# Nine operations stand elsewhere in their engines' sequences, in the recurrence rounds of a fused pool and RWKV block

## What is computed

```python
def rwkv7_branch(ps, mu, ...):
    xs = ps + (token_shift(ps) - ps) * mu
    r, k, v, xw, xa, xg = jnp.split(xs, SHIFT_SPLITS, axis=-1)
    w = -jax.nn.softplus(-(w0 + jnp.tanh(xw) @ w_decay_up)) - 0.5
    decay = jnp.exp(-jnp.exp(w.astype(jnp.float32)))
    a = jax.nn.sigmoid(a0 + xa @ w_aaa_up)
    kk = heads(k * k_k);  kk = kk / jnp.maximum(norm(kk), 1e-12)
    k = k * (1 + (a - 1) * k_a)
    o = wkv7_scan(rh, heads(decay), kh, vh, kk, heads(a))
    ...

def step(state, inp):                      # wkv7_scan, one token
    r_t, w_t, k_t, v_t, a_t, b_t = inp     # a_t = -kk, b_t = kk * a
    sa = jnp.einsum('bhvk,bhk->bhv', state, a_t)
    state = (state * w_t[:, :, None, :] + sa[..., None] * b_t[:, :, None, :]
             + v_t[..., None] * k_t[:, :, None, :])
    return state, jnp.einsum('bhvk,bhk->bhv', state, r_t)
```

## Time and profile before

| what | value |
|---|---|
| time, median of 3 runs | 1096.57 us (1090.94 to 1103.49) |
| the profiled execution's own time | 1097.87 us |
| its span, first to last instruction | 1096.1 us |
| PE busy | 995.9 us (91%) |
| VectorE busy | 520.8 us (48%) |
| ScalarE busy | 413.7 us (38%) |
| GpSimd busy | 402.4 us (37%) |
| mean granted TensorE clock | 0.963 of full |

### The profile page before, as it was taken

One profiled execution on the slowest core, in us unless ns is written; L12 is line 12 of the kernel. 1 busy time (PEld: TensorE's weight loads), 2 busy tenths in 40 slices (PEclk: granted clock), 3 DMA queues, 4 the chain that ended last, 5 costly groups with the idle time before them and its releaser, 6 DMA issues.

```text
span 1096.1 us, 25425 instructions
## 1 busy us (share of the span) xinstructions
PE 995.9 (91%) x10997; PEld 798.7 (73%) x10997; DVE 520.8 (48%) x620; ACT 413.7 (38%) x500; POOL 402.4 (37%) x236
## 2 busy tenths in 40 slices
PE   1798999798989899899899999899999999999992
PEld 1676777685768578766688888678888888888881
DVE  5735688466837867853431246745112112112217
ACT  0336355345435623335432224384124224214311
POOL 6332512310231131125454444355444444443422
PEclk9698999998999999999999999889999999999996
DMA  9332333233222423422443543304333333333201
GB/s 363 103 90 62 97 102 100 61 83 119 86 79 80 119 65 99 116 86 59 135 115 87 165 123 96 96 5 130 97 96 97 96 96 96 96 96 96 77 1 77
DMA packets 153641, 108.08 MB, mean 99 GB/s; under 512 B 5395, under 2 KB 145601, under 8 KB 153537
## 3 DMA queue, kind: packets, MB, share of 16 engines
q1 hardware_dynamic: 143729, 83.46, 26.0%
q10 hardware_dynamic: 9808, 23.08, 6.9%
HBM read 100.23 MB, written 2.10 MB: 93 GB/s over the span
## 4 chain that ended last, share of the span: by engine, by line
PE 75%; DVE 14%; ACT 3%; DMA 2%; issue 2%; POOL 1%; ACTq 1%; SPq 1%; DVEq 0%; POOLq 0%
PE set L1773 23%; PE bank L1773 20%; PE bank L1476 12%; PE set L1518 3%; PE set L1530 2%; PE set L1542 2%; PE bank L1457 2%; PE set L1554 1%; PE bank L1875 1%; DMA ptab<-in_mu_shift_dram 1%; DVE y L1280 1%; DVE Q L1038 1%; PE set L1565 1%; DVE Q L1057 1%; PE set L1875 1%
## 5 line engine op out<-in xcount | busy, mean ns | idle before, releaser
L560 POOL TENSOR_TENSOR w_lo<-w_raw,w_hi 128x1024 fp32r<-128x1024 f32 (+2 forms) x87 | 201.7, 2318 | 441.2 <-ACT w_hi L641 401.1
L616 POOL TENSOR_TENSOR w_lo<-w_raw,w_hi 128x1024 fp32r<-128x1024 f32 x48 | 115.8, 2412 | 145.6 <-ACT w_hi L942 145.4
L1476 PE MATMUL bank<-h_hi,w_hi 128*128 128x512 f32 x256 | 109.3, 427 | 2.2 <-POOL w_lo L560 2.0
L669 ACT ACTIVATE Q<-set 128x1024 f32<-128x1024 f32 x56 | 57.4, 1025 | 135.1 <-PE set L1530 75.6
L641 ACT ACTIVATE w_hi<-w_raw 128x1024 fp32r<-128x1024 f32 (+2 forms) x75 | 75.5, 1006 | 83.0 <-PE set L1773 43.5
L942 ACT ACTIVATE w_hi<-w_raw 128x1024 fp32r<-128x1024 f32 x60 | 63.7, 1061 | 110.7 <-PE bank L1773 53.9
L1476 PE MATMUL bank<-h_lo,w_hi 128*128 128x512 f32 x256 | 104.1, 407 | 0.0
L1476 PE MATMUL bank<-h_hi,w_lo 128*128 128x512 f32 x256 | 103.5, 404 | 0.6 <-issue 0.6
L1371 DVE TENSOR_TENSOR f<-t 128x512 f32<-128x512 f32 x32 | 26.3, 823 | 125.6 <-ACT t L951 125.2
L1773 PE MATMUL set<-y_hi,w_hi 128*128 128x512 f32 x192 | 76.2, 397 | 0.0
L1773 PE MATMUL bank<-h_hi,w_hi 128*128 128x512 f32 x192 | 75.9, 395 | 0.0
(11 more groups left out here) (338 smaller groups left out, 2028.7 us busy)
## 6 DMA issues: line engine op xcount, KB each, us to landing
w_raw<-in_w_ff_dram SPq DMA_DIRECT2D x64, 512.0 KB, 3.9
w_raw<-in_w_in_dram SPq DMA_DIRECT2D x46, 512.0 KB, 3.8
y<-in_w_ada_dram ACTq DMA_DIRECT2D x20, 512.0 KB, 4.2
ada<-in_w_ada_dram SPq DMA_DIRECT2D x16, 512.0 KB, 10.0
Q<-in_w_ada_dram ACTq DMA_DIRECT2D x12, 512.0 KB, 4.3
w_raw<-in_w_rwkv_up_dram SPq DMA_DIRECT2D x8, 512.0 KB, 4.1
w_raw<-in_w_out_dram SPq DMA_DIRECT2D x8, 512.0 KB, 4.0
xtok<-in_x_dram SPq DMA_DIRECT2D x4, 512.0 KB, 10.0
```

What stands on the lines that cost most here:

```text
L560: link(pool.tensor_tensor(part_of(k, w_lo), part_of(k, w_raw), part_of(k, w_hi).bitcast(F32), ALU.subtract), "lo_ready")
L616: again(pool.tensor_tensor(part_of(k, w_lo), part_of(k, w_raw), part_of(k, w_hi).bitcast(F32), ALU.subtract), "lo_ready")
L669: link(act.activation(by_half(tile), psum_flat(set_of(name)), ACT.Copy), "act_kept")
L1476: mm = pe.matmul(o, w, hx, start=(m == 0), stop=(m == 3 * KT - 1))
```

## The change

Nothing is computed otherwise; nine operations move.

- ScalarE: the copy of D goes from slot 10 to slot 9, ahead of the square root L808 and of the fourth load. The issue of the fifth load of w_ada (block 4) goes from the end of slot 11 into slot 12, behind `lora_tanh` and ahead of the copy of K.
- VectorE: A8T plus one goes from slot 8 to slot 7, ahead of the shift and a small copy. `scaled_writes(n, 1)` goes from slot 18 to slot 19, behind the two MR sums. The shift of slot 22 goes to slot 24, behind the fourth state step's add. The use of the last block of w_ada goes from slot 18 to slot 26, behind the last state step's add. One pooling step of round 3 (group 1, last step) goes from slot 6 to slot 7.

```diff
-        ADA_LOADED = (1, 5, 7, 9, 11, 12, 14, 15)
-        ADA_USED = (4, 8, 10, 11, 13, 14, 16, 18)
+        ADA_LOADED = (1, 5, 7, 9, 12, 12, 14, 15)
+        ADA_MIDDLE = 4
+        ADA_USED = (4, 8, 10, 11, 13, 14, 16, 26)
...
-        for g, at in enumerate(((2, 3), (4, 5, 6), (8, 9, 10, 11), (12, 13, 14, 15, 16))):
+        for g, at in enumerate(((2, 3), (4, 5, 7), (8, 9, 10, 11), (12, 13, 14, 15, 16))):
...
+            def load_ada(it, kt):
+                tile = KT * it + kt
+                if it or ada_before(kt):
+                    act.wait_ge(sem("ada2_used"), KT * it + ada_before(kt))
+                if kt == 2:
+                    wait_made(act, "D1", it)
+                act.dma_start(ada_tile(kt), w_ada[0, (tile % KT) * P:(tile % KT + 1) * P, (2 + it) * D:(3 + it) * D]).then_inc(sem(f"ada2_in{int(kt in (2, 4, 6))}"), 16)
...
+                if s == 9 and work:
+                    keep(b6, "D", it)
                 if s == 9 and tail and it < QUADS:
                     act.wait_ge(sem("o_var"), it)
                     link(act.activation(gn[:, 2, :], gn[:, 1, :], ACT.Sqrt), "o_std")
...
-                if s == 10:
-                    if work:
-                        keep(b6, "D", it)
-                    if prep:
-                        squares(it, 1)
+                if s == 10 and prep:
+                    squares(it, 1)
                 if s == 12:
                     if prep:
                         lora_tanh(it, 1)
                     if work:
+                        load_ada(it, ADA_MIDDLE)
                         keep(b1, "K", it)
...
-                if work and s in ADA_LOADED:
-                    kt = ADA_LOADED.index(s)
...
+                if work and s in ADA_LOADED and s != 12:
+                    load_ada(it, ADA_LOADED.index(s))
+                if work and s == 12:
+                    load_ada(it, ADA_MIDDLE + 1)
...
-                at = {1: -1, 7: 0, 10: 1, 16: 2, 18: 3, 22: 4}
+                at = {1: -1, 7: 0, 10: 1, 16: 2, 18: 3, 24: 4}
...
-                if s in (0, 1, 10, 18, 22):
+                if s in (0, 1, 10, 18):
                     if s == 18 and work:
                         keep_pair(b1, b2, "AP1", it)
                     project(it, s)
-                    if s == 18 and prep:
-                        scaled_writes(n, 1)
...
                     if work:
                         keep_masked(c6, c8, mKR, "KR0", it)
                         keep_masked(c6, c8, mKR, "KR1", it)
+                        keep_plus_one(b5, "A8T", "A8T", it)
                     project(it, s)
                     if prep:
                         chunk_decay(n, 0)
-                if s == 8:
-                    if work:
-                        keep_plus_one(b5, "A8T", "A8T", it)
...
                     keep_sums(b4, b6, b4, Rt, "MR0", it)
                     keep_sums(b4, b6, b4, Rt, "MR1", it)
+                if s == 19 and prep:
+                    scaled_writes(n, 1)
...
                     keep(dve.tensor_tensor(state, ps, state, ALU.add), f"S{at}", it)
+                if s == 24:
+                    project(it, s)
```

## The result

The changed kernel takes 1089.73 us (median of 20 runs, 1083.93 to 1097.95); the kernel before took 1097.68 beside it. The ratio is 0.9934, interval 0.9913 to 0.9954: 7 us faster, not 22. One of the 20 executions of the kernel before took 1707.8 us; why is not known, and the ratio is of the others. The profiled execution took 1089.25 us with a span of 1087.5, so 8.6 are to be explained between it and the one shown of before.

A forecast was written before the change was run, and what follows sets the result against it. PE's list was taken to bound rounds 0 to 3, with only its idle time and low-clock stretches to win; 5.7, 8.0, 5.5 and 3.1 us by round make 22.3, so 1097.9 becomes 1076, range 1067 to 1088.

The forecast's parts named there:

- D's copy and the load: ScalarE, rounds 0 to 2: yT 5.4 us earlier in round 1 (3.0 if the clock drops), 3.55 in round 2.
- A8T ahead of the shift: VectorE, rounds 0 to 2: A8T comes 0.95 us earlier for PE's inv0; gain 0.9, 0.5 and 1.0 us.
- MR sums: VectorE, rounds 0 to 2: sums taken once MR0 is made, OI follows N unwaited; 6.6 us in three rounds.
- `rt_made` held by GpSimd: Ahead of S1's add: GpSimd's product holds the pair once a round, 3.00 us instead of 1.4.
- The shift: State steps S1 to S6, rounds 0 and 1: gain 3.2 and 3.7 us, less 0.9 if low clock comes.
- Round 2: Whole round: 3.55 us, then 5.95 at S1's add, less 0.4, so 5.5 us faster.
- Round 3: Pooling step behind A8T (W0 2.2 us earlier), no 1.86 before K, but yT waits for KI: 3.1 us faster.
- (b): Rival: half given back, `rt_made` held by both products (6.0 us), state steps at low clock (4.5); 1086, chance 0.15.
- (c): Rival: waits hide another bound, such as VectorE's list in slots 14 to 20; 1089, chance 0.07.

The follow-up runs named there:

- the second execution: The changed kernel, unaltered, measured and profiled once more: 1090.15 us, ratio 0.9927 to the kernel before; its profiled time was 1080.71 us.

## Why the prediction was wrong

**The step that failed** is in its first paragraph: "only two things can be won there, PE's idle time [...] and stretches at the low clock", with each wait then booked as won in full, as in "OI follows N with no wait: 1.84 us in this round, 6.6 in three". There was a third term, PE's supply of instructions: 12.5 us over the four rounds in the profiled execution, 8.2 in the second. It stood in the rows of before at 7.6 us, as idle for issue in the midst of products, and I read it as part of the idle time and not as a limit that sits behind the data waits. Taking the waits away brought it up.

- **D's copy and the load.** Right: HD1's wait is 1.27 (predicted 1.1), twice, and KI's new wait before yT 0.87 (predicted 0.8). 2.4 us a round each. The run with this part alone is as fast as the whole change, though only 2.4 us of it show as less idle time.
- **A8T ahead of the shift.** inv0 no longer waits for it; round 0 has 0.54 and round 2 0.85 for issue close by, round 1 nothing.
- **MR sums.** The wait went; the gain didn't come. In round 2, 2.47 for the sums became 2.45 for issue. The run with this part alone, 0.9998, shows that this term of 6.6 us was worth 2.7 us at the very most (0.9975).
- **`rt_made` held by GpSimd.** Wrong, and in my favour: 3.0 us a pair was expected, and it took 1.4 in all three rounds. GpSimd's products wait for OI, OI ended later than in my timetable because of its stalls (without the 0.38 and 1.36 of round 1 the product would have started at 285.9, inside `rt_made`), and VectorE was through. Timelines of VectorE and GpSimd of after, round 1 and round 0:

```profile
285.56 1.42 DVE L1266 TENSOR_TENSOR Q<-G 128x512 f32<-128x512 f32 x2
```

```profile
192.20 2.31 POOL L594 TENSOR_TENSOR Q<-Q,DC 128x1024 f32<-128x1024 f32 x1 [5.14 <-PE set L1535]
```

  In round 0 `rt_made` starts at 191.33, and ends 0.5 us behind the product's start. In round 1 the product starts at 287.66, behind it.
- **The shift.** The steps took what was predicted, 7.57 and 7.55 us. Of 6.8 us, 2.9 went at the next two stalls in the run with this part alone.
- **Round 2.** Predicted 5.5 faster, measured 0.1, and 1.5 in the second execution. The waits went as predicted, but 2.45 and 0.85 for issue came, the first stall of the round grew from 1.16 to 2.55, and PE's busy time was 1.8 more at granted clock 0.97 where before had 0.98.
- **Round 3.** Predicted 3.1 faster, measured 4.9 slower, but 2.4 faster in the second execution (88.0 against 90.4), so most of this miss is of one execution. W0 was to be 2.2 earlier; the wait for the pooling step (1.0) is gone, but the stall 12 matmuls ahead of that product's end grew from 0.57 to 2.40. K's 1.86 is gone and KI is waited for 2.31 instead. From S6's add of round 2 to yT it took 57.6 us (395.17 to 452.73) and 53.1 before (411.52 to 464.64), with 6.6 us for issue in it and 1.4 before. Four stalls (1.94, 1.27, 2.40, 1.92) come to 7.5 where 2.5 stood; in the second execution they come to 2.7 (none, 0.84, 0.48, 1.38).
- **Rivals.** (b), 1086, had nearly the size and the wrong reason: no hold by GpSimd, no low clock in the state steps. (c), another bound that the waits hide, 1089, had the size and the right kind, but by luck: it named VectorE's list, whose place PE's own supply takes, and it had a chance of 0.07 and lay outside the range. The range ended at 1088, below the measured 1089.73.

## What to carry to other kernels

Idle time of the bounding engine that is named issue, and stands in the midst of a run of like instructions, is a limit of its own and not slack: before a wait is booked as won, count the instructions behind it, and look whether a run of small ones (here over 128 of 64 columns) starves the supply. Then a data wait there is partly free, and taking it away gives little. Wide instructions set into the run take away most of the idle for issue (20.0 to 7.8 us), but they cost some 0.35 us each by themselves and uncover what they had covered: 2 to 4 us of 1090 were left here, not told apart for sure. ScalarE's part, whose main waits stand among wide matmuls, brought 1.3 us of new idle for issue where the other two parts brought 5.3 and 6.0; that the wide ones are the reason is not shown. And take the same kernel's profile twice before you explain a single round by it.

## What the runs showed of the hardware

- PE takes small float32 matmuls (64 columns) at 128 in 3.5 to 3.7 us in a stretch that waits for nothing, where they themselves need 2.1; with 128 columns most blocks follow without a stop and the steady stop is 0.30 us, at three places of 16 blocks. 2048 of either kind took about as long, 59.0 and 60.3 us. From a block's packet to the next matmul it was 2.3 to 2.7 us in eight places of two kernels.
- The queue moved one packet of 16 KB for 128 matmuls and their 128 weight loads (32 packets for 4096).
- Where a stall can stand is fixed by the sequence, its length isn't: 0.48 and 2.40 us at the same matmul in two executions of the same kernel.
- Four wide matmuls between narrow ones cost PE some 0.35 us more than four more in a run of wide ones (1.28 us for a run of four, 3.10 for twelve).
